# Grouped attention: where the query projection is evacuated and where its products stand

## What is computed

```python
q = (h @ w_q).reshape(B, S, SW_KV_HEADS, SW_GROUP, HEAD_DIM)
q = apply_rope(rms_norm(q, q_norm), cos, sin)
s = einsum('bnqhgd,bnkhd->bnhgqk', qb, kw) * scale       # keys: own block and the one before
m = maximum(max(s), sink); e = exp(s - m)
p = e / (sum(e) + exp(sink - m))
o = einsum('bnhgqk,bnkhd->bnqhgd', p, vw)
return o.reshape(B, S, -1) @ w_o
```

## Time and profile before

| what | us |
|---|---|
| median of 3 runs (3098.01 to 3102.64) | 3100.03 |
| the profiled execution | 3097.99 |
| its span | 3096.1 |
| first grouped attention, without context, loop | about 844 to 1008 |
| second, with context, loop | about 2429 to 2651 |

### The profile page before, as it was taken

How to read it: one execution, slowest core, us unless ns; L and a number is a source line. 1 busy time by engine, 2 the same in 40 slices (tenths; PEclk the granted TensorE clock), 3 DMA queues, 4 the chain that set the end, 5 groups by cost and what they waited for, 6 DMA issues and landing times.

```text
span 3096.1 us, 41620 instructions
## 1 busy us (share of the span) xinstructions
PE 2809.8 (91%) x14244; PEld 2346.1 (76%) x14244; DVE 1686.2 (54%) x2544; ACT 1269.5 (41%) x2121; POOL 639.9 (21%) x298
## 2 busy tenths in 40 slices
PE   4999899997687899997987899999997898899998
PEld 4777687886666777886876788888886787688886
DVE  5777544445665444435996464354455455464645
ACT  3444365644355364654211233132233465352422
POOL 0111087873011087873000000000000000000000
PEclk9999899998799899998997899999998999999999
DMA  3111244542100244443111111121111000222221
GB/s 121 42 44 59 82 161 168 174 156 103 41 25 18 82 169 164 170 161 104 55 49 34 55 55 61 62 68 62 60 46 46 28 28 8 69 85 92 96 94 63
DMA packets 67905, 252.07 MB, mean 81 GB/s; under 512 B 7456, under 2 KB 8736, under 8 KB 64928
## 3 DMA queue, kind: packets, MB, share of 16 engines
q1 hardware_dynamic: 67744, 249.99, 23.8%
HBM read 247.87 MB, written 2.10 MB: 81 GB/s over the span
## 4 chain that ended last, share of the span: by engine, by line
PE 44%; issue 21%; DVE 19%; POOL 7%; ACT 6%; DVEq 2%; ACTq 1%; DMA 0%; POOLq 0%
PE psum L1682 11%; PE psum L1681 11%; PE psum L1683 11%; POOL mod_p L485 7%; DVE work L1205 4%; DVE w_lo L1081 2%; DVE work L1310 1%; PE psum L2037 1%; ACT work L870 1%; PE psum L1820 1%; ACT w_hi L568 1%; DVE hx_lo L1304 1%; ACT sw_pt L882 1%; PE psum L1798 1%; PE psum L1799 1%
## 5 line engine op out<-in xcount | busy, mean ns | idle before, releaser
L1081 DVE TENSOR_TENSOR w_lo<-w_raw,w_hi 128x1024 fp32r<-128x1024 f32 (+3 forms) x334 | 451.3, 1351 | 412.6 <-ACT w_hi L568 400.3
L1681 PE MATMUL psum<-hx_hi,w_hi 128*128 128x512 f32 x1568 | 623.6, 398 | 30.0 <-DVE w_lo L1081 14.0
L1682 PE MATMUL psum<-hx_lo,w_hi 128*128 128x512 f32 x1568 | 624.8, 398 | 0.0
L1683 PE MATMUL psum<-hx_hi,w_lo 128*128 128x512 f32 x1568 | 623.3, 398 | 0.0
L485 POOL TENSOR_TENSOR mod_p<-mod_w,mod_c 128x1024 f32<-128x1024 f32 x192 | 547.7, 2884 | 186.1 <-ACT mod_p L553 150.7
L568 ACT ACTIVATE w_hi<-w_raw 128x1024 fp32r<-128x1024 f32 (+3 forms) x334 | 356.3, 1067 | 271.9 <-PE psum L1683 216.6
L475 POOL TENSOR_TENSOR tok_r<-tok_ms,half 128x4 f32<-128x4 f32 (+1 forms) x70 | 71.8, 1026 | 1857.9 <-DVE tok_ms L1005 1246.2
L1681 PEld LDWEIGHTS psum<-hx_hi,w_hi 128*128 128x128 f32 x1568 | 296.9, 189 | 81.7 <-issue 16.6
L1683 PEld LDWEIGHTS psum<-hx_hi,w_lo 128*128 128x128 f32 x1568 | 296.8, 189 | 70.3
L1682 PEld LDWEIGHTS psum<-hx_lo,w_hi 128*128 128x128 f32 x1568 | 297.4, 190 | 48.5
L1681 PE MATMUL psum<-a_hi,w_hi 128*128 128x512 f32 (+1 forms) x656 | 233.5, 356 | 18.6 <-DVE a_lo L1146 10.3
(11 more groups left out here) (263 smaller groups left out, 4972.3 us busy)
## 6 DMA issues: line engine op xcount, KB each, us to landing
mod_w<-in_w_mod SPq DMA_DIRECT2D x96, 512.0 KB, 3.6
w_raw<-in_fup SPq DMA_DIRECT2D x88, 512.0 KB, 4.5
w_raw<-in_cup SPq DMA_DIRECT2D x88, 512.0 KB, 3.5
w_raw<-in_fdown SPq DMA_DIRECT2D x32, 512.0 KB, 4.7
w_raw<-in_cdown SPq DMA_DIRECT2D x32, 512.0 KB, 3.4
w_raw<-in_da_qkv SPq DMA_DIRECT2D x8, 1536.0 KB, 6.4
w_raw<-in_fdown SPq DMA_DIRECT2D x16, 384.0 KB, 4.6
w_raw<-in_cdown SPq DMA_DIRECT2D x16, 384.0 KB, 3.0
```

Of the source, the lines that this page charges most:

```text
L1081: dve.tensor_tensor(w_lo[:, off:off + n], w_raw[:, raw:raw + n], w_hi[:, off:off + n].bitcast(F32), ALU.subtract).then_inc(s_lo, 1)
L1681: pe.matmul(dst, wh, xh, start=first, stop=False)
L1682: pe.matmul(dst, wh, xl, start=False, stop=False)
L1683: return pe.matmul(dst, wl, xh, start=False, stop=last)
```

## The change

On ScalarE `evac_proj` leaves the odd step (unit m+3, behind the exponentials) and stands at the head of the next even step (unit m+2 of the new m, the same unit). On TensorE the first two of the four k-steps of each half always stand behind `turn` and `turn_q`, and the second two always behind `values(p-1, 0)` (and behind `turn(p-1, 2)` where there is one). That was TensorE's order already where `parts` is 2 or 3. The number of units, their instructions and their waits stay as they are.

```diff
--- before.py
+++ after.py
@@ -920,8 +920,8 @@
                 for p in range(34):
                     m, half = p // 2, p % 2
                     parts = len(chunks(st, p - 1)) if 0 < p < 33 else 0
-                    if p == 0:
-                        evac_proj(2)
+                    if half == 0 and m < 14:
+                        evac_proj(m + 2)
                     if half and m:
                         spread_out(m - 1)
                     if parts:
@@ -934,8 +934,6 @@
                         exps(p, 1)
                     if parts > 2:
                         weights(p - 1, 2)
-                    if half and m < 13:
-                        evac_proj(m + 3)
                     if half and m < 16:
                         sinks(m)
                     if half and m < 14:
@@ -2059,8 +2057,6 @@
                     k0 = 4 * half
                     if p < 32:
                         scores(p)
-                    if parts == 1 and m < 13:
-                        project(m + 3, k0, k0 + 2)
                     if parts:
                         turn(p - 1, 0)
                     if parts > 1:
@@ -2068,12 +2064,12 @@
                     if half and m < 14:
                         turn_q(m + 2)
                     if m < 13:
-                        project(m + 3, k0 + 2 if parts == 1 else k0, k0 + 4 if parts == 1 else k0 + 2)
+                        project(m + 3, k0, k0 + 2)
                     if parts:
                         values(p - 1, 0)
                     if parts > 2:
                         turn(p - 1, 2)
-                    if parts != 1 and m < 13:
+                    if m < 13:
                         project(m + 3, k0 + 2, k0 + 4)
                     for c in range(1, parts):
                         values(p - 1, c)
```

## The result

The changed kernel takes 3078.33 us (4 runs, 3073.29 to 3079.83), the kernel before 3099.08 (4 runs, 3098.01 to 3102.64). The medians are 20.7 us apart. The ratio on record, 0.9928 with a 95% interval of 0.9913 to 0.9943, is not exactly the quotient of the two medians (0.9933); its interval means 18 to 27 us. The forecast started from 3100.03, the median of three runs; the fourth run took the median of the kernel before to 3099.08, and that accounts for 0.95 us of the distance.

What follows compares the result with a forecast made beforehand. Without context a VectorE-ScalarE chain was taken to bound grouped attention, with context nearly TensorE's queue; gains of 7.6 and 6.0 us, 13.6 together, gave 3086.5 us on the median's footing, range 3081 to 3094.5.

Steps and rivals of the forecast that it cites:

- The loop in A: Grouped attention without context: VectorE and ScalarE alternate; moving `evac_proj` shortens each of 13 rounds by 0.74 us, 9.6 in all.
- my step list: TensorE's new order in a round without context: `project` waits for the evacuation, odd scores still reach VectorE in time.
- The slack of 0.8 us: Attention without context: margin between TensorE's odd scores and VectorE taking them up, absorbing the new wait before `project`.
- The exceptions in A: Attention without context: two weight-refill rounds with slow TensorE fall 0.3 and 1.7 us short, leaving some 7.6 us.
- B: Grouped attention with context, nearly TensorE's own queue: 7 odd steps gain 0.6 us, 6 gain 0.45, about 6.0 us altogether.
- The bound of 8 us: Attention with context: most the stage could gain, if all of the even half's TensorE waits go.
- One stage only: Rival: new TensorE hand-overs cost more, the stage without context gains 1 us, the other 6.0; 3093 us, chance 0.16.
- It changes nothing: Rival: ScalarE's new order only shifts which engine waits; 3098 to 3100 us, chance 0.10.
- The clock falls: Rival: longer TensorE idle before the even `project`, without context, lowers the clock; 3114 us at seven slow rounds, chance 0.07.
- the short listed wait of the even `project`: Sign expected on TensorE: `project` in the even half shows a short wait for ScalarE's evacuation (L854).

Runs made afterwards that it cites:

- odd_doubled: Kernel before with two more copies in each `evac_proj`, left at its old place in the odd step; 3132.22 us, 1.0108 to the kernel before.
- even_doubled: Changed kernel with two more copies in each `evac_proj`, at its new place in the even step; 3086.42 us, 0.9962 to the kernel before.
- scalar_only: Kernel before with only ScalarE's `evac_proj` moved, in both stages, TensorE's order as before; 3086.33 us, 0.9949 to the kernel before.
- stage_b_only: Kernel before with `evac_proj` moved only in the attention stage with context, TensorE's order as before; 3087.15 us, 0.9952 to the kernel before.
- stage_a_only: Kernel before with both parts of the change only in the attention stage without context; 3090.15 us, 0.9964 to the kernel before.
- changed_again: The same changed kernel timed again later, beside other runs of the kernel before (3096.96 us); 3076.11 us, 0.9933.
- turn_q_later: Changed kernel with TensorE's `turn_q` placed behind the first two k-steps of `project`, in both stages; 3076.87 us, 0.9928 to the kernel before.

## Why the prediction was right in sign and short in size

**The loop in A: right.** The round went from 10.28 to 9.48 us, `q_low` waits 1.64 us, L860 took the time it was given, and the old place costs 0.45 us a copy (`odd_doubled`) while the new one is free to within 0.2 (`even_doubled`). I priced the move at 0.74 us, from 955.32 to 956.06; it was 0.80. The sinks now follow the exponentials after 0.09 us, as `evac_proj` followed them after 0.14, so the small gap went too.

**TensorE in A, by my step list: right.** I put the even `project` at +2.35 us after the exponentials, `values` at +3.1, the odd scores at +5.25, their reading at +6.97. With 938.74 (938.55 and 0.19) as the end of the exponentials, the trace has +2.32, +3.13, +5.17 and +6.91. The slack of 0.8 us held, and no round was lost. `scalar_only` shows that it comes from TensorE's half of the edit: without it seven of 13 rounds miss it.

**The exceptions in A: the first failed step.** I took 2.0 us off for the two refill rounds, where TensorE came out slow before. They shortened by 0.80 and 0.79 us like all others. In the stretch where the earlier trace rows has a clock of 0.59 the changed kernel has none. Over 12 us, before and after:

```profile
880.00:892.00 12.00, 9.98 (x60) 9.01 (x60) 7.28 (x22) 6.75 (x20) 1.65 (x2) 0.86 0.00 0
```

```profile
880.00:892.00 12.00, 10.25 (x71) 9.00 (x71) 7.05 (x22) 8.34 (x25) 1.65 (x2) 1.00 0.00 0
```

The slow stretch is not tied to its place. `stage_b_only` has the code of before in A and starts it 3.49 us later; in the matching 12 us its clock is 1.00:

```profile
883.49:895.49 12.00, 8.88 (x60) 7.45 (x60) 7.26 (x22) 6.76 (x20) 1.65 (x2) 1.00 0.00 0
```

And there it cost the kernel before nothing: the round that holds it took 9.47 us, and 9.46 in `stage_b_only`. Where a slow stretch came in a round of one key tile in a profile of the changed A (`stage_a_only`, 889 to 895 us), that round took 9.24 us in place of 8.66:

```profile
889.00:895.00 6.00, 6.00 (x40) 5.61 (x39) 4.38 (x12) 3.10 (x10) 1.65 (x2) 0.81 0.00 0
```

So its price there is 0.6 us where I allowed 1.7, and it is not paid in every profile. What one costs in a refill round of the changed kernel no run shows, since none came there. 13 times 0.80 is 10.4 us against the forecast's 7.6.

**B: the second failed step.** I gave 0.6 us to 7 rounds and 0.45 to 6, less 0.9 for the first two, 6.0 us. Measured from one spread of the inverses to the next on TensorE, five rounds are 0.80 to 0.91 us shorter and five 0.45 to 0.54; the first is 0.73 shorter, the last two 1.34 and 0.61, with the slow stretch of the profile of before in them (0.86 and 0 against `stage_a_only`, which has none). So 0.45 was right, 0.6 was a third too small, and the 0.9 taken off was wrong, since the first two gave 0.73 and 0.53. The bound of 8 us was too low with them: the stage gave 8.5. I had sized it by the listed wait of 0.64 us before 2486.49. The starts say more. TensorE of before at that place, around the row of 2486.49 in the earlier trace rows:

```profile
2485.34 0.28 PE L1956 MATMUL psum<-w_hi,hx_hi 128*128 128x256 f32 x1
...
2485.58 0.28 PE L1958 MATMUL psum<-w_hi,hx_lo 128*128 128x256 f32 x1
...
2487.46 0.61 PE L2044 MATMUL psum<-ident,inv_wide 128*128 128x128 f32 x4
```

and the same instructions in the changed kernel:

```profile
2475.23 0.28 PE L1954 MATMUL psum<-w_hi,hx_hi 128*128 128x256 f32 x1
...
2475.46 0.28 PE L1956 MATMUL psum<-w_hi,hx_lo 128*128 128x256 f32 x1
2475.58 1.02 PE L2035 MATMUL psum<-sw_pt,sw_va 128*128 128x256 f32 x4
2476.44 0.61 PE L2042 MATMUL psum<-ident,inv_wide 128*128 128x128 f32 x4
```

From the last k-step's first product to `values` there were 1.15 us (2485.34 to 2486.49), now 0.35: 0.80 us gone where 0.64 were listed. The idle time is counted from the end that the trace gives the product before (2485.58 and 0.28, to 2486.49), and a group that does not wait starts before that end: at 2475.58, where the product before ends at 2475.74. That is the missing 0.16. From `values` to the spread it is 0.97 and 0.86, another 0.11. Together 0.91 us, the whole difference of that round (12.76 to 11.85), of which the listed wait had shown seven tenths. The Trainium skill, "Perfetto Trace Analysis", section "Tensor Engine Instruction (MATMUL, LD_WEIGHTS)", says that TensorE's end in a trace is a model, worked out from the instruction's size; this is what it costs an estimate that reads waits and not starts.

**The sum.** The terms I had are 7.6 and 6.0, 13.6 us. Measured, they are 10.3 and 8.5, 18.8 us. Of the 5.2 us that were missing, about 2.5 are B, 2.0 the refill rounds, and 0.8 the 0.80 us a round where I had 0.74. The remaining 2 us up to the 20.7 (20.9 in `changed_again`) are within the interval of the ratio, which starts at 18 us. They are also of the size of the slow stretches that the profile of before had and that of after had not, 1.1 us in each stage; whether the other runs of the kernel before had them too, no run here shows.

**The rivals.** *One stage only* falls: `stage_a_only` and `stage_b_only` are 10.0 and 13.0 us below the kernel before. *It changes nothing* falls with the lengths of the stages, and with `odd_doubled`, where the old place costs each copy in full. *The clock falls* did not happen: the granted clock over A is 0.97 where it was 0.94, 1.00 over B, and the pauses of TensorE in 936 to 948 us, the new order's round, leave it at 1.00. The slow stretches that the changed kernel has in A begin at 974 us, behind the 13 rounds. The case that the rule of small idles between matmul groups bears out (the Trainium skill, "TensorE: Matmul & The Clock Gate", "A second HAM failure mode: psum-queue depth-cycling"), was the one of 3114 us; here the trace does not agree with the rule for the rounds, and the row was the better guide. Of the signs I named, the short listed wait of the even `project` is listed in 9 of the 13 rounds (0.26 to 1.26 us); in the plain round shown the evacuation comes just in time.

## What to carry to other kernels

When a round is closed by a chain of two engines, what stands between the hand-overs costs its full time each round (0.45 us a copy here), and the same work behind the hand-over costs little or nothing up to the wait that it lands in (0 to 0.2 us for two copies): read that wait first, then look which queue consumes the moved result and move its consumer by as much, since either half alone can lose. Size a TensorE wait by the spacing of starts with and without it, not by the idle time in brackets. Take no term for a slow clock stretch from one profile; look at a second one of an unchanged stage first.

## What the runs showed of the hardware

A listed TensorE wait of 0.64 us stood for 0.80 us of delay at its place. The slow clock stretches of A come and go between programs whose code there is the same (880 to 892 us has 0.86 before, the matching stretch of `stage_b_only` has 1.00). Inside a plain round they cost nothing (before), 0.3 us (`turn_q_later`, a round of 8.99 us where others have 8.65) or 0.6 (`stage_a_only`), not the 1.7 I expected. In the end of the stage TensorE's stretch was 5 us longer at 0.69 than at 0.86; that the clock alone makes the difference is likely and not shown. And the beginning of A varies from 842.5 to 850.5 us between profiles of programs that do not differ ahead of it. That spread is larger than the effect of any of the single moves, which is why stage lengths tell these moves apart and medians do not.
